# Sparse attention's opening: the first two score steps ahead of the first two gate projections, with gates and value blocks in banks of their own

## What is computed

```python
def nsa_mixer(h, positions, w_in, b_gate, pe_k, pe_v, ck_w1, ck_w2, cv_w1, cv_w2, w_out):
    p = (h @ w_in).astype(jnp.float32)
    q, kc, vc, ks, vs, kw, vw, gl, z = jnp.split(p, splits, axis=-1)
    ...                                              # rope of q, kc, ks, kw
    kcmp = compress(kc, pe_k, ck_w1, ck_w2)          # 31 compressed keys
    vcmp = compress(vc, pe_v, cv_w1, cv_w2)
    ...
        s = jnp.einsum('bghtd,bgcd->bghtc', qb, kcmp)
        pc = jax.nn.softmax(jnp.where(valid, s, NEG), axis=-1)
        o_c = jnp.einsum('bghtc,bgcd->bghtd', pc, vcmp)
        ...                                          # o_s: keys of chosen blocks, o_w: keys of a window
    gates = jax.nn.sigmoid(gl + b_gate.astype(jnp.float32)).reshape(B, S, NSA_HEADS, 3)
    o = jnp.einsum('bshc,bshcd->bshd', gates, out).reshape(B, S, NSA_Q) * jax.nn.silu(z)
    return o @ w_out.astype(jnp.float32)
```

## Time and profile before

| | |
|---|---|
| median of 3 runs | 2099.21 us (2096.14 to 2102.98) |
| profiled execution | 2099.4 us, its span 2097.2 us |
| TensorE busy | 1995.9 us, 95% of the span |
| VectorE, ScalarE busy | 1070.1 us (51%), 892.7 us (43%) |
| GpSimd busy | 222.5 us (11%) |
| DMA | 169.93 MB, mean 81 GB/s |

### The profile page before, as it was taken

The page is one execution under the profiler, slowest core; times in us unless marked ns, Lnnn a source line. Parts: engine busy times, 40 slices in busy tenths (PEclk is TensorE's granted clock), DMA queues, the critical chain, the costliest instruction groups (busy, mean ns, idle before and its releaser), DMA issues. The chain is left out here.

```text
span 2097.2 us, 27351 instructions
## 1 busy us (share of the span) xinstructions
PE 1995.9 (95%) x11189; PEld 1603.3 (76%) x11189; DVE 1070.1 (51%) x1706; ACT 892.7 (43%) x1653; POOL 222.5 (11%) x225
## 2 busy tenths in 40 slices
PE   7999889999999999999999999999999899899988
PEld 6778778888887787657888888877887778756567
DVE  5676565343435443674544443546345754455763
ACT  5561354322314653674432232455244522245552
POOL 1010000000000000440000000000000143133440
PEclk9999999999999999999999999999999999999999
DMA  5221013333322132111332233212321256301001
GB/s 153 70 80 42 24 61 108 101 101 100 99 89 88 66 110 81 41 41 61 111 101 81 100 101 101 81 62 95 101 71 41 85 169 185 106 21 33 9 2 70
DMA packets 122481, 169.93 MB, mean 81 GB/s; under 512 B 7482, under 2 KB 83654, under 8 KB 122358
## 3 DMA queue, kind: packets, MB, share of 16 engines
q1 hardware_dynamic: 114502, 150.47, 22.2%
q0 software_dynamic: 5504, 14.58, 2.6%
q10 hardware_dynamic: 2352, 3.15, 0.4%
HBM read 158.22 MB, written 2.10 MB: 76 GB/s over the span
## 5 line engine op out<-in xcount | busy, mean ns | idle before, releaser
L412 DVE TENSOR_TENSOR WL<-RAW,WH 128x1024 fp32r<-128x1024 f32 (+1 forms) x283 | 347.6, 1231 | 371.6 <-ACT WH L482 371.2
L482 ACT CAST WH<-RAW 128x1024 fp32r<-128x1024 f32 (+1 forms) x283 | 292.7, 1037 | 381.0 <-PE PSUM L516 380.9
L516 PE MATMUL PSUM<-XH,WH 128*128 128x512 f32 (+4 forms) x1128 | 421.1, 373 | 15.9 <-DVE XL L412 5.3
L516 PE MATMUL PSUM<-XL,WH 128*128 128x512 f32 (+4 forms) x1128 | 413.4, 367 | 0.0
L516 PE MATMUL PSUM<-XH,WL 128*128 128x512 f32 (+4 forms) x1128 | 413.1, 366 | 0.0
L516 PE MATMUL PSUM<-WH,HP 128*128 128x512 f32 x1024 | 317.9, 390 | 1.9 <-DVE WL L412 1.9
L516 PEld LDWEIGHTS PSUM<-XH,WH 128*128 128x128 f32 (+3 forms) x1128 | 211.4, 187 | 56.8 <-DVE XL L412 10.4
L516 PE MATMUL PSUM<-WH,XH 128*128 128x512 f32 (+1 forms) x608 | 238.9, 393 | 16.5 <-DVE WL L412 10.3
L516 PEld LDWEIGHTS PSUM<-XL,WH 128*128 128x128 f32 (+3 forms) x1128 | 211.4, 187 | 36.6 <-issue 2.9
L516 PEld LDWEIGHTS PSUM<-XH,WL 128*128 128x128 f32 (+3 forms) x1128 | 211.3, 187 | 35.0
L516 PE MATMUL PSUM<-WL,XH 128*128 128x512 f32 (+1 forms) x608 | 231.5, 381 | 0.0
(11 more groups left out here) (236 smaller groups left out, 2484.0 us busy)
## 6 DMA issues: line engine op xcount, KB each, us to landing
RAW<-in_w_mlp_dram SPq DMA_DIRECT2D x64, 1024.0 KB, 5.2
RAW<-in_nsa_w_in_dram SPq DMA_DIRECT2D x14, 1024.0 KB, 5.1
RAW<-in_w_in_e_dram SPq DMA_DIRECT2D x12, 1024.0 KB, 5.3
RAW<-in_w_qkv_o_dram SPq DMA_DIRECT2D x12, 1024.0 KB, 5.1
RAW<-in_gla_w_in_dram SPq DMA_DIRECT2D x12, 1024.0 KB, 5.1
RAW<-in_w_ple_gate_dram SPq DMA_DIRECT2D x8, 1024.0 KB, 5.0
RAW<-in_w_out_e_dram SPq DMA_DIRECT2D x4, 1024.0 KB, 5.0
RAW<-in_w_out_o_dram SPq DMA_DIRECT2D x4, 1024.0 KB, 5.0
```

What stands on the lines that cost most here:

```text
L412: return x.do.tensor_tensor(o, a, b, op)
L482: a.do.copy(hi, r).then_inc(*up("w_hi", "w_hi", j))
L516: m = p.do.matmul(o, l, r, start=start and i == 0, stop=stop and i == len(pairs) - 1)
```

## The change

Scores 0 go directly behind the compression and scores 1 behind nz 0; nz 0 goes into bank 7, nz 1 into bank 6, the value blocks into bank 5. ScalarE and VectorE follow in the same order. The mask's two casts move ahead, into the step of the first window keys. In `feat` the unused argument `keep` gives way to `bank`.

```diff
@@ -560,12 +560,12 @@
                 if (before + i + 1) % count == 0:
                     yield
 
-        def feat(p, job, n, kind="F", keep=False):
+        def feat(p, job, n, kind="F", bank=None):
 
             for t in range(4):
                 x_whole(p, n, t)
             j, hi, lo = part(p, kind)
-            b = ps.take(*job, keep=keep)
+            b = ps.take(*job, bank=bank)
             p.wait_ge(*at("w", j))
             p.wait_ge(*ps.empty(*job))
             chain(p, PS[b][0:hi.shape[2], :], three(lambda k: (hi[:, k, :], lo[:, k, :]), xs_feat, 8)).then_inc(
@@ -2519,17 +2519,6 @@
                         chain(p, PS[b][:, 0:128], [(W2D[:, m, :, :].rearrange("p e d -> p (e d)"), HD[:, 0, m, :])
                                                    for m in range(2)]).then_inc(*ps.filled(*job))
                     compress(br)
-            feat(p, ("nz", 0), NSA)
-            b = ps.take("vcb")
...
-            m.then_inc(*ps.filled("vcb"))
-
             def scores(u):
                 f, q, br, m0 = n_at[u]
                 n, nk = BESIDE[q], 128 * (q + 1)
@@ -2624,9 +2613,23 @@
                 if 0 <= i < 24:
                     next(rest)
 
+            def value_blocks():
+                b = ps.take("vcb", bank=5)
+                p.wait_ge(*ps.empty("vcb"))
+                p.wait_ge(*at("w2_v"))
+                for g in range(4):
+                    p.wait_ge(*at("r4", g))
+                    r4 = tm("r4", g)[:, 0:256].rearrange("p (k e c) -> p k e c", k=2, e=4)
+                    m = chain(p, PS[b][:, 64 * g:64 * g + 64], [(r4[:, m, :, :].rearrange("p e c -> p (e c)"), W2[:, 1, m, :])
+                                                                for m in range(2)])
+                m.then_inc(*ps.filled("vcb"))
+
             step_(-2)
-            feat(p, ("nz", 1), NSA)
-            for i in range(-1, NT - 2):
+            feat(p, ("nz", 0), NSA, bank=MORE)
+            step_(-1)
+            value_blocks()
+            feat(p, ("nz", 1), NSA, bank=ACC)
+            for i in range(NT - 2):
                 step_(i)
             toks(p, ("yo", 1, 0), mixed_ready, head=True, mid=[lambda: step_(NT - 2), lambda: step_(NT - 1), lambda: step_(NT)],
                  tiles=TILES[1], banks=(0, 1, 2, 3))
@@ -2674,8 +2677,6 @@
                 act(a, z, z, ACT.Exp, scale=-1.0).then_inc(*up("nz_sig", "nz_sig", m))
                 act_weights(a, first_part["nz", m] + 3)
 
-            z_gate(0)
-
             def exps(u):
                 f, q, br, m0 = n_at[u]
                 a.wait_ge(*at("negmax", u))
@@ -2718,8 +2719,10 @@
                 nsa_step(i, ((turn_, 0), (exps, 2)))
 
             step_(-2)
+            z_gate(0)
+            step_(-1)
             z_gate(1)
-            for i in range(-1, NT + 2):
+            for i in range(NT + 2):
                 step_(i)
             j = first_part["yo", 1, 0]
             act_weights(a, j + 5)
@@ -2800,6 +2803,9 @@
                         v.wait_ge(*at("w2_k"))
                         v.do.tensor_copy(W2D[:, :, 0, :], W2[:, 0, :, :])
                         v.do.tensor_copy(W2D[:, :, 1, :], W2[:, 0, :, :]).then_inc(*up("w2_twice", "w2_twice"))
+                        v.wait_ge(*at("c_nsa"))
+                        v.do.tensor_copy(IDB, IDT)
+                        v.do.tensor_copy(NMB, NM[:, 384:512]).then_inc(*up("mask", "mask"))
                 else:
                     if i in pieces:
                         gather(*pieces[i])
@@ -2823,11 +2829,12 @@
                 tt(v, z, bank("nz", m)[:, :], z, ALU.mult).then_inc(*ps.read("nz", m))
                 dve_weights(v, first_part["nz", m] + 3)
 
-            z_gate(0)
-            v.wait_ge(*ps.full("vcb"))
-            for g in range(4):
-                m = tt(v, VC[:, g, :, :], b1(bank("vcb")[:, 64 * g:64 * g + 64], 4), b2(CN[:, N_BD:N_BD + 4], 64), ALU.mult)
-            m.then_inc(*ps.read("vcb"))
+            def value_blocks():
+                v.wait_ge(*ps.full("vcb"))
+                for g in range(4):
+                    m = tt(v, VC[:, g, :, :], b1(bank("vcb")[:, 64 * g:64 * g + 64], 4), b2(CN[:, N_BD:N_BD + 4], 64),
+                           ALU.mult)
+                m.then_inc(*ps.read("vcb"))
 
             def most(u):
                 f, q, br, m0 = n_at[u]
@@ -2902,12 +2909,12 @@
                 if 0 < i <= 24 and i % 4 == 0:
                     z_gate(1 + i // 4)
 
-            v.wait_ge(*at("c_nsa"))
-            v.do.tensor_copy(IDB, IDT)
-            v.do.tensor_copy(NMB, NM[:, 384:512]).then_inc(*up("mask", "mask"))
             step_(-2)
+            z_gate(0)
+            step_(-1)
+            value_blocks()
             z_gate(1)
-            for i in range(-1, NT + 2):
+            for i in range(NT + 2):
                 step_(i)
             j = first_part["yo", 1, 0]
             dve_weights(v, j + 5)
```

More of the change, by code:

```diff
@@ L2521, in pe_nsa @@
                     compress(br)
-            feat(p, ("nz", 0), NSA)
-            b = ps.take("vcb")
-            p.wait_ge(*ps.empty("vcb"))
-            p.wait_ge(*at("w2_v"))
-            for g in range(4):
[L2527 to L2530, removed]
-            m.then_inc(*ps.filled("vcb"))
             def scores(u):
```

## The result

The changed kernel takes 2090.99 us (median of 15 runs, 2088.00 to 2095.41), the kernel before 2099.83 (15 runs, 2095.61 to 2104.92): 8.8 us less by the medians, ratio 0.9964 with a 95% interval of 0.9954 to 0.9974. The forecast was 2088.7, 10.7 us less. The range of 2084.0 to 2093.5 held the time; the narrower span that the forecast gave by its own prices, 2087.5 to 2090, did not. The profiled execution of the changed kernel has a span of 2088.8 us, 8.4 under that of before.

What follows compares the result with a forecast made beforehand. TensorE was taken to set the time, with 10.0 us idle and 5.7 us clock loss in the opening. Turn 1 12.3 us earlier less 1.6 for the clock gives 10.7: 2099.4 to 2088.7 us, range 2084.0 to 2093.5.

Steps and rivals of the forecast that it cites:

- The timetable: Opening from 1807.40: row prices laid out per engine put turn 1 at 1830.4 instead of 1842.72, 12.3 us earlier.
- The new wait: TensorE ahead of turn 1: stands 3.7 us, 1826.7 to 1830.4, as scale 1 queues behind gate 1 and step 2's max.
- bank 7's 0.46 us wait: Gate 0's projection behind the compression: ScalarE still reads bank 7; scores 0 hide it, otherwise it costs 0.3 us.
- the 0.7 us: VectorE's weight subtraction slowed beside a GpSimd share: would add 0.7 us to the wait; by the timetable neither meets one.
- the clock: Half-clock work behind the wait ahead of turn 1: takes back 1.6 us, bounds 0 and 3.2.
- the rest of the span stays as it is: Turn 1 to the end: 254.5 us before, forecast the same plus the clock's 1.6 us.
- A sign of being wrong: The prediction is wrong if turn 1 to the end grows by more than 3 us, or a second wait precedes turn 1.
- rival 2: More is lost: two half-clock stretches (2090.3), collision, casts, a wait between steps; 2090.3 to 2092.5 us, chance 0.14.
- the forecast's own case: Whole kernel: 10.7 us saved, 2088.7 us (2087.5 to 2090 by its own prices), chance 0.58.
- the casts: Mask casts moved ahead on VectorE into the first window keys' step: costed at nothing, at most 0.4 us.
- Rival 3: Gain given back later: waits for GpSimd at thirteen later turns (7.0 us) grow; 2096 to 2099 us, chance 0.09.
- rival 4: Slower: clock stays at 0.50 through the steps behind the new wait; 2105.7 us with 37 us of half-clock work, chance 0.04.

Runs made afterwards that it cites:

- r5: Changed kernel with VectorE's scale of step 1 moved directly behind the value blocks; 2088.08 us, ratio 0.9947 to the kernel before.
- r3: Kernel before, old order, with only both gates and the value blocks moved to banks 7, 6 and 5; 2094.06 us, ratio 0.9973 to the kernel before.
- r4: Changed kernel with the score matmuls of step 3 issued four times, filling TensorE's wait ahead of turn 1; 2090.03 us, ratio 0.9948 to the kernel before.
- r2: Changed kernel's new order, but gates and value blocks take banks from the deal again (0, 1, 2); 2097.99 us, ratio 0.9985 to the kernel before.
- r1: The changed kernel measured again, on the chip on which its variants run; 2092.05 us, ratio 0.9959 to the kernel before.
- r6: Changed kernel with the output projection's four token tiles in banks 3, 2, 1, 0 instead of 0, 1, 2, 3; 2087.69 us, ratio 0.9941 to the kernel before.
- r7: Changed kernel with both the early scale of step 1 and the output projection's banks turned; 2081.23 us, ratio 0.9916 to the kernel before.

## Why the prediction was right, and where its size was off

**The timetable held.** Scores 0 to turn 0 ran without a wait (turn 0 starts at 1823.94; the timetable had it at 1823.8). The new wait was forecast ahead of turn 1, 3.7 us long up to 1830.4, and is 3.51 long up to 1830.51. The saving up to there was forecast as 12.3 us and is 12.2. Its cause, scale 1 behind gate 1 and the max of step 2 on VectorE, is shown by r5.

**What was moved at no cost cost nothing.** The table load stands at 1810.19 on ScalarE, ahead of the compressed exponential, under nz 0; bank 7's 0.46 us wait (forecast as 0.3 if uncovered) appears only in r3, where the cover is taken away. VectorE and ScalarE in the opening, after:

```profile
1817.25 1.23 DVE L412 TENSOR_TENSOR WL<-RAW,WH 128x1024 fp32r<-128x1024 f32 x1 [0.24 <-ACT WH L482]
...
1825.85 1.23 DVE L412 TENSOR_TENSOR WL<-RAW,WH 128x1024 fp32r<-128x1024 f32 x1 [0.25 <-ACT WH L482]
1826.99 1.22 DVE L2844 TENSOR_REDUCE ST<-PSUM 128x2 f32<-128x1024 f32 x1
```

```profile
1810.19 1.28 ACT L425 ACT_TABLE_LOAD   x1 [2.34 <-DVE AR L412]
```

Both weight subtractions took 1.23 us, not the 1.93 of the earlier trace rows: none met a share, as the timetable said, and the 0.7 us were rightly left out of the sum.

**The mis-sized term is the clock.** I took 1.6 us for the one new idle piece, from the piece of 2.83 us as the nearer row. In the trace it cost 2.5, which was the other row of the same sentence (the piece of 5.38 us), and r4 gives 2.4 for it as a difference between two kernels. It lies within the upper bound that I set, 3.2 for two stretches of the short kind. The earlier trace rows had also cut the edges of the stretches. From change to change of the clock they are 6.8, 3.4 and 3.4 us long, the first of them, before:

```profile
1818.60:1825.40 6.80, 5.16 (x24) 0.50 0.48 154
```

So 6.0 us were lost to the clock in the opening before, and not 5.7, and the full-clock work is 19.3 us, just what the timetable adds up to. And the sentence that the rest of the span stays as it is was wrong by 1.3 us: near 2031 the same idle piece drew 6.8 us at half clock instead of 3.4. Together 12.2 - 2.5 - 1.3 = 8.4, the difference of the two spans. Whether the change makes the second loss likelier, or it is chance, stays open: the same work and the same 2.8 us idle were followed by 3.4 us at half clock (before, r2), 6.8 (after, r1, r5) and none (r3, r4).

**A sign of being wrong came.** The prediction called itself wrong if the time from turn 1 to the end, 254.5 us before, grew by more than 3 us. It grew by 3.8, to 258.3 (2088.8 less 1830.51), and not by the 1.6 forecast: 0.9 more at turn 1 and 1.3 more near 2031. The stretch at half clock, forecast at 3.3 us, was 6.8. The timetable was right and the price of the clock was not; the range held the time because it was drawn to cover rival 2 as well.

**The rivals.** Rival 2, more is lost (0.14), describes what came better than the forecast's own case (0.58): its two half-clock stretches of the short kind put the time at 2090.3 and its range ends at 2092.5, and 2090.99 lies between. Its other causes, the collision on VectorE and the casts, did not come. Rival 3 did not come: behind turn 1 TensorE waits for GpSimd at the full turns 13 times and 6.9 us in all, where it was 13 times and 7.0, and the last of these waits is shifted by 9.7 us. No stretch at half clock behind turn 1 is longer than 6.8 us, so rival 4, the slower side, stays without support.

## What to carry to other kernels

Where an engine waits for "a bank", look whose product lies in it. Here a projection and the value blocks happened to be dealt the banks of the next scores, and moving them alone gave more than the order alone (5.9 us against 2.0, and 7.9 for both). Lay out a timetable from rows for each engine in turn before moving work; it gave the new wait to 0.2 us, and reading its cause (a short operation queued behind long ones that nobody awaits yet) gave the next gain at once. Price each idle piece of TensorE that is left with its share of half clock as well, as a range and not as one value, and once for every idle piece downstream.

## What the runs showed of the hardware

Idle time of TensorE has an after-cost that depends on where it falls. In these traces stretches at half clock at an idle piece came as 3.4 us or 6.8 us or not at all, for one and the same piece of 2.8 us. Even a piece of 2.0 us drew 3.4 us in four traces of nine. The 3.5 us piece of the changed kernel drew 6.8 us in all three traces that have it with its banks (after, r1, r6), and 3.4 in r2. Filling such a piece with work that has no use (r4) brought what follows 2.4 us forward, in the one trace that was taken of it.

The spread between executions goes with the clock as well. The opening starts at 1807.4 to 1807.5 in two traces (before, after) and at 1811.04 in r1, with almost the same code ahead of it (only the mask's two casts moved). TensorE's clock, the kernel before and then r1:

```profile
230.00:240.00 10.00, 8.22 (x115) 1.00 0.00 1
298.00:306.00 8.00, 7.89 (x40) 1.00 0.41 131
1455.00:1475.00 20.00, 16.58 (x66) 0.91 0.28 97
```

```profile
230.00:240.00 10.00, 8.58 (x113) 0.83 0.01 2
298.00:306.00 8.00, 6.96 (x28) 0.79 0.44 131
1455.00:1475.00 20.00, 16.56 (x63) 0.83 0.19 58
```

In r1 the clock also falls near 234 and 300 us and for longer near 1460, each time at places where the other trace has it higher. Over everything ahead of the opening that makes 34 us at half clock instead of 24, and r1 reaches the opening 3.6 us later, some 40% of what this change gives. The other traces fall into the same two groups: r5 and r7 have 24 us at half clock and begin the opening at 1806.9 and 1806.7, and r2, r3, r4 and r6 have 34 and begin it at 1811.0 to 1812.0. The times agree: of the 23 executions of the kernel before that stand beside r1 to r4, the four with a mean granted clock of 0.991 took 2095.5 to 2096.1 us, and the nine with 0.987 took 2100.9 to 2104.0. That the clock is the cause of the spread is read from these numbers, and no run tried it.
